# The remainders of the normalised rows: both halves on GpSimd in the closing stages

## The chip, the cores and the metric

The kernel runs on one core of one Trainium2 chip. A core has TensorE (matrix products, transposes), VectorE, ScalarE and GpSimd (elementwise work), and SyncE, whose queue here issues the weight loads. The metric is the device time of one launch in microseconds. Engines run their own instruction streams in order; they meet only at semaphores, on which an instruction waits until a count is reached.

## The reference

One inference step of a backbone with two layers over 640 tokens (128 context tokens, 512 latent tokens, width 1024). Each sub-layer is wrapped in the same chain, and this chain is what the change touches:

```
hp = modulate(rmsnorm(xp, norm_mix_pre[layer]), mod_p[0], mod_p[1])
...                                   # mixer: gMLP + RG-LRU (layer 0), attention (layer 1)
xp = xp + mod_p[2] * rmsnorm(yp, norm_mix_post[layer])
xs = xs + mod_s[2] * rmsnorm(ys, norm_mix_post[layer])
hp = modulate(rmsnorm(xp, norm_ffn_pre[layer]), mod_p[3], mod_p[4])
hs = modulate(rmsnorm(xs, norm_ffn_pre[layer]), mod_s[3], mod_s[4])
xp = xp + mod_p[5] * rmsnorm(sq_relu_mlp(hp, w_ffn_in[layer], w_ffn_out[layer]), norm_ffn_post[layer])
```

All matrix products are of fp32 precision. They are made of three products of a rounded part (type fp32r) and a remainder: high by high, high by low, low by high.

## The kernel before

Tokens are worked on in five tiles of 128 rows (t = 0 to 4). `X` holds the residual stream, `ACC` the sub-layer's sum and later the normalised rows, `HF` the modulated and transposed rows of one token tile in fp32, `HH` its rounded part and `HL` the remainder `HF - HH`, with features on the partitions. `HH` and `HL` are what the next projection multiplies with the weights (`WH`, `WL`, made from `RAW` in a ring of six blocks).

The host code writes one list of steps by hand (`schedule`), and every engine walks through that list and issues its own part of each step, so the list sets the order on every engine. A token tile closes a sub-layer in these steps:

- `post` (ScalarE L859, L860; VectorE L1226, L1228, L1230): mean square of the sub-layer's output, gain, residual add into `X`; signals `x_new`.
- `pre` (ScalarE L869, L870; VectorE L1234, L1235): the norm of `X`, the normalised rows into `ACC`; signals `xn_ready`.
- `T`: TensorE transposes the rows into two PSUM banks (L1602). VectorE evicts the first bank with the modulation into `HF[:, 0:4]` (L1259, four instructions); before that it waits for `h_lo[0]`, the remainder of the first half of the tile before, since there is one `HF`.
- `cut`: ScalarE waits for `h_lo[1]` of the tile before, evicts the second bank into `HF[:, 4:8]` (L890, four instructions), then rounds the halves into `HH` (L895, L897), and signals `h_hi` after each. VectorE forms the remainder of the first half (L1265), GpSimd that of the second (L1058).

`normed(ph, t)` puts these together while the last projection of a sub-layer still runs, two tiles behind: `T` of tile t-2, `post` of t, `cut` of t-2, `pre` of t. Tiles 3 and 4 are left over; `ffn` issues their `T` and `cut` back to back after the first 256 token columns of the first product (`tiles(0, 0)`, which needs the remainders of two tiles), and follows with a modulation product (`mod`, L1544) and the other 384 columns, for which TensorE waits for both halves of all five tiles (`input_ready`, both `h_lo`). There are three closings of this kind: the output projection of layer 0, the last MLP chunk of layer 0, where tiles 3 and 4 are turned between the `qkv` products, and the output projection of layer 1. So each of the three has five cuts, 15 in all.

GpSimd's queue holds, besides the remainders of `HL`, the splits of the weights into `WL` (L1068, two instructions of 128x512 for each block) and, in the attention, the scaling of the weights (L1053), all in the order of the list. ScalarE rounds the weights (L812), and evicts in several stages (L985, L991, L939).

Of the kernel before, what the change touches and what calls it, by code (L numbers as in the profile page):

```python
# [17 lines left out]
P = 128  # L18
# [390 lines left out]
def key_tiles(t):  # L409

    if t == 0:
        return [0]
    return sorted([TT] + list(range(max(1, t - 1), min(LAT, t + 1) + 1)), key=key_slot)
# [17 lines left out]
def hybrid_step(nc, A):  # L431
    f32, f32r, bf16 = mybir.dt.float32, mybir.dt.float32r, mybir.dt.bfloat16
    ALU, ACT, AX = mybir.AluOpType, mybir.ActivationFunctionType, mybir.AxisListType
# [3 lines left out]
    with ctx:  # L437
        def sb(name, shape, dt=f32):
            return ctx.enter_context(nc.sbuf_tensor(name, shape, dt))
# [6 lines left out]
        def sem(name):  # L446
            return ctx.enter_context(nc.semaphore(name))
# [3 lines left out]
        HH = sb("HH", [P, KD, TOK], f32r)  # L451
        HL = sb("HL", [P, KD, TOK], f32r)
# [11 lines left out]
        HF = sb("HF", [P, KD, P])  # L464
# [101 lines left out]
        h_hi = sem("h_hi")  # L566
        h_lo = [sem(f"h_lo{i}") for i in range(2)]
# [65 lines left out]
        def weights_of(i):  # L633

            if i < NKV:
                return GGF[:, 2048 + 512 * i:2560 + 512 * i].rearrange("p (h n) -> p h n", h=4)
            return Z[:, i % 2, :, :]
# [33 lines left out]
        def pt_copies(eng, copy, i, who):  # L671

            for q, (unit, kt, by, _) in enumerate(PT_TILES):
                if unit == i and by == who:
                    upto(eng, pt_mm, q)
                    if i:
                        upto(eng, m_ready, PV_M[i - 1])
                    copy(weights_t(i, kt), PS[:, 4 + q % 2, :]).then_inc(pt_ready[who], 1)  # L678

        def w_view(ld, b):  # L680

            place = raw(ld)
            k = LOADS[ld]["kind"]
            if k == "acols":
                return place.rearrange("p (k n) -> p k n", k=KD)[:, :, P * b:P * b + P]
            return place[:, 1024 * b:1024 * b + 1024]

        def ring_view(buf, ld, j):
            k = LOADS[ld]["kind"]
            if k == "acols":  # L690
                return buf[:, j % RING, :].rearrange("p (k n) -> p k n", k=KD)
            return buf[:, j % RING, :]
# [55 lines left out]
        @block.sync  # L748
        def _(sp):
            for t in range(TT):  # L750
                rows = A["x_prompt"][0] if t == 0 else A["x_sample"][0, (t - 1) * P:t * P, :]
                sp.dma_start(X[:, t, :], rows).then_inc(x_in[t], 16)
            for i, ld in enumerate(LOADS):
                if i in EARLY:
                    sp.dma_start(raw_dst(i, ld), dram_view(ld)).then_inc(early_in[i], 16)
                    continue
                if RAW_NO[i] >= RAWN:

                    old = LOADS[RAW_LD[RAW_NO[i] - RAWN]]
                    if old["kind"] == "mod" and old["vec"] is not None:  # L760
                        sp.wait_ge(vec_read, 4 * old["vec"] + 2 * old["kh"] + 2)
                    elif old["kind"] == "mod" and old["kh"] == 0:
                        sp.wait_ge(mod_read, old["n"] + 1)
                    elif old["kind"] == "mod":
                        upto(sp, m_ready, old["m"])
                    else:
                        sp.wait_ge(w_lo, old["first"] + 2)
                    if i == PT_LOAD + RAWN:
                        upto(sp, m_ready, PV_M[-1])
                sp.dma_start(raw_dst(i, ld), dram_view(ld)).then_inc(raw_in[RAW_NO[i] % RAWN], 16)  # L770

            for t in range(TT):
                sp.wait_ge(x_new, 3 * TT + t + 1)
                dst = A["y_prompt"][0] if t == 0 else A["y_sample"][0, (t - 1) * P:t * P, :]
                sp.dma_start(dst, X[:, t, :]).then_inc(stored, 16)
            sp.wait_ge(stored, 16 * (2 + TT))
            sp.wait_ge(k_out, 16)
# [264 lines left out]
        @block.gpsimd  # L1042
        def _(pool):
            for s in STEPS:
                k = s["kind"]
                if k == "sums":

                    i, z = s["n"], s["n"] % 2
                    nk = P * len(key_tiles(s["t"]))
                    pool.wait_ge(sum_ready, i + 1)  # L1050
                    inv = AST[:, z, 5, :].unsqueeze(2).broadcast_to([P, 4, nk])
                    w = weights_of(i)[:, :, 0:nk]
                    nc.gpsimd.tensor_tensor(w, w, inv, ALU.mult).then_inc(p_ready, 1)  # L1053
                if s["kind"] == "cut":
                    t = s["t"]
                    pool.wait_ge(h_hi, 2 * s["n"] + 2)
                    cols = slice(t * P, t * P + P)
                    nc.gpsimd.tensor_tensor(HL[:, 4:8, cols], HF[:, 4:8, :], HH[:, 4:8, cols].bitcast(f32), ALU.subtract)\  # L1058
                        .then_inc(h_lo[1], 1)
                if k == "B" and s["what"] == "u" and s["t"] == TT - 1:  # L1060
                    pool.wait_ge(h_sum, 3)
                for j, _ in s["split"]:
                    ld, b = BLOCK_LOAD[j]
                    pool.wait_ge(w_hi, j + 1)
                    for piece in (0, 1):
                        cut = (lambda v: v[:, 4 * piece:4 * piece + 4, :]) if LOADS[ld]["kind"] == "acols" else \
                            (lambda v: v[:, 512 * piece:512 * piece + 512])
                        ins = nc.gpsimd.tensor_tensor(cut(ring_view(WL, ld, j)), cut(w_view(ld, b)),  # L1068
                                                      cut(ring_view(WH, ld, j)).bitcast(f32), ALU.subtract)
                    ins.then_inc(w_lo, 1)  # L1070
# [3 lines left out]
        def _(dve):  # L1074
            own = [0]
            V_ = nc.vector
# [70 lines left out]
            for s in STEPS:  # L1147
                k = s["kind"]
# [65 lines left out]
                elif k == "post":  # L1214
                    ph, t = s["ph"], s["t"]
# [15 lines left out]
                elif k == "pre":  # L1231
                    ph, t = s["ph"], s["t"]
# [18 lines left out]
                elif k == "T":  # L1251
                    ph, t, u0 = s["ph"], s["t"], s["m"]
# [6 lines left out]
                        ins = V_.tensor_scalar(HF[:, f, :], m_bank(u0)[:, P * f:P * f + P], MODC[:, layer, off + 1, f, v:v + 1],  # L1259
                                               MODC[:, layer, off, f, v:v + 1], ALU.mult, ALU.add)  # L1260
                    ins.then_inc(m_free[u0 % 2], 1)
                elif k == "cut":
                    cols = slice(s["t"] * P, s["t"] * P + P)
                    dve.wait_ge(h_hi, 2 * s["n"] + 1)
                    V_.tensor_tensor(HL[:, 0:4, cols], HF[:, 0:4, :], HH[:, 0:4, cols].bitcast(f32), ALU.subtract).then_inc(h_lo[0], 1)  # L1265
                elif k == "A":
                    if s["what"] == "xr" and s["fin"] and s["tile"] == 2:
                        conv(dve, V_, link, 0, 0)
# [65 lines left out]
                elif k == "B":  # L1334
                    b, t, nb, what = s["b"], s["t"], s["nb"], s["what"]
# [4 lines left out]
                elif k == "rope":  # L1340

                    t, nb, b = s["t"], s["nb"], s["group"]
                    bank = PS[:, 4 + b % 2, :]
                    heads = 8 if nb < 2 else NKV
                    n = heads * HD
# [35 lines left out]
                elif k == "G2":  # L1381
                    t, c = s["t"], s["c"]
# [55 lines left out]
                elif k == "ya":  # L1438
                    u, t = s["m"], s["t"]
# [4 lines left out]
                elif k == "softmax":  # L1444
                    i, t, z = s["n"], s["t"], s["n"] % 2
# [40 lines left out]
        def _(pe):  # L1486
# [36 lines left out]
            for s in STEPS:  # L1523
# [120 lines left out]
                elif k == "B":  # L1644
                    b, t, nb, what = s["b"], s["t"], s["nb"], s["what"]
                    b_acquire(b)
                    if what == "wout":
                        if s["ph"] == 1 and nb == 0:
                            upto(pe, m_free, YA_M[t])
                        if s["ph"] == 3 and nb == 0:  # L1650
                            upto(pe, m_free, PV_M[NKV * t + 2])
                            upto(pe, m_free, PV_M[NKV * t + 3])
                        if s.get("pt"):
                            before = pv_steps(TT * NKV - 2)
                            for q in (before - 2, before - 1):
                                if q % 2 == b % 2:
                                    _, _, by, count = PT_TILES[q]
                                    pe.wait_ge(pt_ready[by], count)
                    elif what == "qkv":
                        input_ready(pe, TT + (t + 1 if nb == 2 else TT))  # L1660
# [101 lines left out]
                elif k == "PV":  # L1762
# [15 lines left out]
                    def transposed(kt):  # L1778
                        q = base + kt
                        if q >= 2:  # L1780
                            _, _, by, count = PT_TILES[q - 2]
                            pe.wait_ge(pt_ready[by], count)
                        for h in range(4):
                            ins = TR(PS[:, 4 + q % 2, P * h:P * h + P], weights_of(i)[:, h, P * kt:P * kt + P], IDN[:, :])  # L1784
                        ins.then_inc(pt_mm[q % 2], 1)
# [64 lines left out]
```

## Time and profile before

| | |
|---|---|
| median of 3 runs | 1503.34 us (1503.22 to 1504.46) |
| profiled execution | 1500.87 us, span 1499.1 us |
| TensorE busy | 1422.2 us, 95% |
| VectorE, ScalarE, GpSimd busy | 717.2, 545.7, 549.4 us |
| DMA | 153.76 MB, mean 103 GB/s |

The span runs from the first to the last instruction of the profiled execution. Busy is the time in which an engine has an instruction under way; TensorE's instructions overlap each other, so its busy time is not time at its peak.

### The profile page before, as it was taken

Reading aid. Unit: us, or ns where it says so; the run is one execution under the profiler, and the core shown is the slowest. Engines: PE = TensorE matmul, PEld = TensorE weight load, DVE = VectorE, ACT = ScalarE, POOL = GpSimd, SP = SyncE. Lnnn points to the kernel's source line nnn. Section 1 sums busy time; section 2 is a strip of 40 time slices with the busy share of each in tenths; the row PEclk is TensorE's granted clock in tenths of the full one; section 3 lists DMA queues with packets and bytes.
Section 4 is the critical chain, followed back from the end, with each engine's and each line's share of the span. In section 5 each row is a group of like instructions: output and inputs, shape, how many; then the busy total and the mean of one; then the engine's idle time right before and its main releaser. Section 6 shows DMA issues by size and latency. Waiting matters only on the chain.

```text
span 1499.1 us, 19717 instructions
## 1 busy us (share of the span) xinstructions
PE 1422.2 (95%) x7958; PEld 1205.9 (80%) x7958; DVE 717.2 (48%) x1274; ACT 545.7 (36%) x912; POOL 549.4 (37%) x383
## 2 busy tenths in 40 slices
PE   5999999899999999999899889998999999999998
PEld 3876877789889899898667755677989989989986
DVE  5477945532544544545834677617323223222236
ACT  4467706522122122123631466628312212222222
POOL 1431404534244244244334234433624424433430
PEclk8999999999999999999999999999999999999999
DMA  9524253345334234233425000030534213213201
GB/s 353 144 94 143 86 193 104 112 128 112 108 104 141 90 108 141 87 111 119 162 90 170 28 1 1 1 112 29 165 103 127 65 48 113 80 44 103 85 28 71
DMA packets 95026, 153.76 MB, mean 103 GB/s; under 512 B 10764, under 2 KB 49368, under 8 KB 94936
## 3 DMA queue, kind: packets, MB, share of 16 engines
q1 hardware_dynamic: 82432, 145.76, 29.7%
q10 hardware_dynamic: 12504, 6.75, 1.8%
q8 instruction: 63, 1.03, 0.3%
q14 instruction: 27, 0.22, 0.0%
HBM read 149.58 MB, written 2.92 MB: 102 GB/s over the span
## 4 chain that ended last, share of the span: by engine, by line
PE 76%; DVE 8%; ACT 4%; issue 2%; POOL 2%; DMA 2%; DVEq 0%; ACTq 0%
PE PS L1493 23%; PE PS L1495 23%; PE PS L1494 23%; POOL WL L1068 2%; PE PS L1792 1%; PE PS L1784 1%; PE PS L1544 1%; DVE GG L1458 1%; DVE X L1230 1%; PE PS L1642 1%; PE PS L1759 1%; DVE XCB L1226 1%; ACT WH L812 1%; DVE HL L1265 1%; DVE RAW L678 1%
## 5 line engine op out<-in xcount | busy, mean ns | idle before, releaser
L1068 POOL TENSOR_TENSOR WL<-RAW,WH 128x512 fp32r<-128x512 f32 x340 | 468.3, 1413 | 719.3 <-ACT WH L812 701.7
L1493 PE MATMUL PS<-HH,WH 128*128 128x384 f32 (+1 forms) x1152 | 357.9, 311 | 8.4 <-POOL HL L1058 3.6
L1495 PE MATMUL PS<-HH,WL 128*128 128x384 f32 (+1 forms) x1152 | 356.2, 309 | 0.0
L1494 PE MATMUL PS<-HL,WH 128*128 128x384 f32 (+1 forms) x1152 | 356.1, 309 | 0.0
L812 ACT CAST WH<-RAW 128x1024 fp32r<-128x1024 f32 x170 | 169.1, 1047 | 445.3 <-PE PS L1495 331.2
L1493 PE MATMUL PS<-WH,AH 128*128 128x512 f32 x640 | 250.4, 391 | 0.3 <-DVE AL L1282 0.3
L1495 PE MATMUL PS<-WH,AL 128*128 128x512 f32 x640 | 249.5, 390 | 0.0
L1494 PE MATMUL PS<-WL,AH 128*128 128x512 f32 x640 | 249.3, 390 | 0.0
L1493 PEld LDWEIGHTS PS<-HH,WH 128*128 128x128 f32 x1152 | 218.9, 190 | 16.7 <-issue 10.3
L1494 PEld LDWEIGHTS PS<-HL,WH 128*128 128x128 f32 x1152 | 219.1, 190 | 0.6
L1495 PEld LDWEIGHTS PS<-HH,WL 128*128 128x128 f32 x1152 | 218.7, 190 | 0.0
L1301 DVE TENSOR_TENSOR XCB<-XCB 128x640 f32<-128x640 f32 x60 | 70.1, 1168 | 270.7 <-ACT XCB L939 270.4
L1389 DVE TENSOR_TENSOR ACC<-ACC,PS 128x512 f32<-128x512 f32 x140 | 95.8, 686 | 171.8 <-PE PS L1495 171.8
L1493 PEld LDWEIGHTS PS<-WH,AH 128*128 128x128 f32 x640 | 120.2, 188 | 27.4 <-issue 3.3
L1495 PEld LDWEIGHTS PS<-WH,AL 128*128 128x128 f32 x640 | 120.1, 188 | 25.3
L1494 PEld LDWEIGHTS PS<-WL,AH 128*128 128x128 f32 x640 | 120.2, 188 | 24.3
L1493 PE MATMUL PS<-WH,HH 128*128 128x512 f32 x280 | 112.7, 403 | 1.1 <-DVE GG L1353 0.9
L1495 PE MATMUL PS<-WH,HL 128*128 128x512 f32 x280 | 109.9, 393 | 0.0
L1494 PE MATMUL PS<-WL,HH 128*128 128x512 f32 x280 | 109.8, 392 | 0.0
L939 ACT ACTIVATE XCB<-PS 128x640 f32<-128x640 f32 x60 | 42.3, 705 | 163.1 <-PE PS L1495 163.1
L1053 POOL TENSOR_TENSOR GG<-GG,AST 128x1536 f32<-128x1536 f32 (+2 forms) x20 | 55.0, 2748 | 90.3 <-DVE AST L1475 90.3
L1303 DVE TENSOR_TENSOR AL<-XCB,AH 128x640 fp32r<-128x640 f32 x60 | 53.4, 890 | 47.6 <-ACT AH L945 47.6
(210 smaller groups left out, 1624.0 us busy)
## 6 DMA issues: line engine op xcount, KB each, us to landing
RAW<-in_w_mod SPq DMA_DIRECT2D x43, 1024.0 KB, 5.1
RAW<-in_w_ffn_in SPq DMA_DIRECT2D x32, 1024.0 KB, 5.5
RAW<-in_w_ffn_out SPq DMA_DIRECT2D x32, 1024.0 KB, 4.9
RAW<-in_w_in_even SPq DMA_DIRECT2D x7, 1024.0 KB, 5.3
RAW<-in_w_qkv SPq DMA_DIRECT2D x6, 1024.0 KB, 5.2
RAW<-in_w_out_even SPq DMA_DIRECT2D x4, 1024.0 KB, 5.1
GG<-gates ACTq DMA_DIRECT2D x16, 256.0 KB, 3.8
RAW<-in_w_out_odd SPq DMA_DIRECT2D x4, 1024.0 KB, 5.9
```

Of the source, the lines that this page charges most:

```text
L678: copy(weights_t(i, kt), PS[:, 4 + q % 2, :]).then_inc(pt_ready[who], 1)
L812: nc.scalar.copy(ring_view(WH, ld, j), w_view(ld, b)).then_inc(w_hi, 1)
L939: nc.scalar.activation(XC[0], a_bank(a), ACT.Relu).then_inc(a_free[a % 2], 1)
L1053: nc.gpsimd.tensor_tensor(w, w, inv, ALU.mult).then_inc(p_ready, 1)
L1068: ins = nc.gpsimd.tensor_tensor(cut(ring_view(WL, ld, j)), cut(w_view(ld, b)), cut(ring_view(WH, ld, j)).bitcast(f32), ALU.subtract)
L1226: V_.tensor_tensor(YG, ACC[:, t, :], gain, ALU.mult).then_inc(yg_ready, 1)
L1301: V_.tensor_tensor(XC[1], XC[0], XC[0], ALU.mult).then_inc(sq_ready, 1)
L1303: V_.tensor_tensor(AL[:, slot, :], XC[1], AH[:, slot, :].bitcast(f32), ALU.subtract).then_inc(a_lo, 1)
L1389: V_.tensor_tensor(acc, acc, bank, ALU.add).then_inc(b_free[b % 2], 1)
L1493: MM(out, wh, xh, start=first, stop=False)
L1494: MM(out, wh, xl, start=False, stop=False)
L1495: return MM(out, wl, xh, start=False, stop=last)
```

## The change

In every `cut` the remainder of the first half moves from VectorE to GpSimd. GpSimd now waits for the first half's rounding, forms the first remainder, waits for the second rounding and forms the second remainder. VectorE has nothing left in `cut`, neither the wait nor the subtraction. The signals `h_lo[0]` and `h_lo[1]`, and all who wait for them, stay as they are. The steps' order, the number of instructions and the arithmetic are the same.

```diff
@@ gpsimd @@
                 if s["kind"] == "cut":
                     t = s["t"]
+                    cols = slice(t * P, t * P + P)
+                    pool.wait_ge(h_hi, 2 * s["n"] + 1)
+                    nc.gpsimd.tensor_tensor(HL[:, 0:4, cols], HF[:, 0:4, :], HH[:, 0:4, cols].bitcast(f32), ALU.subtract)\
+                        .then_inc(h_lo[0], 1)
                     pool.wait_ge(h_hi, 2 * s["n"] + 2)
-                    cols = slice(t * P, t * P + P)
                     nc.gpsimd.tensor_tensor(HL[:, 4:8, cols], HF[:, 4:8, :], HH[:, 4:8, cols].bitcast(f32), ALU.subtract)\
                         .then_inc(h_lo[1], 1)
@@ vector @@
-                elif k == "cut":
-                    cols = slice(s["t"] * P, s["t"] * P + P)
-                    dve.wait_ge(h_hi, 2 * s["n"] + 1)
-                    V_.tensor_tensor(HL[:, 0:4, cols], HF[:, 0:4, :], HH[:, 0:4, cols].bitcast(f32), ALU.subtract).then_inc(h_lo[0], 1)
```

## Rows read from the trace of the kernel before

**Rows 1.** The page: busy time (share) xinstructions of each engine; the ending chain's shares.
```profile
PE 1422.2 (95%) x7958; PEld 1205.9 (80%) x7958; DVE 717.2 (48%) x1274; ACT 545.7 (36%) x912; POOL 549.4 (37%) x383
...
PE 76%; DVE 8%; ACT 4%; issue 2%; POOL 2%; DMA 2%; DVEq 0%; ACTq 0%
```

**Rows 2.** By source line: the two remainders, min/median/max ns, first and last start.
```profile
L1265 DVE TENSOR_TENSOR HL<-HF,HH x15: 691/1764/1794, 255.4 to 1049.0; 128x512 fp32r<-128x512 f32 x15
...
L1058 POOL TENSOR_TENSOR HL<-HF,HH x15: 1261/1458/1648, 255.2 to 1049.6; 128x512 fp32r<-128x512 f32 x15
```

**Rows 3.** Timeline of VectorE, first closing: start, length, line, [idle before <-releaser].
```profile
257.32 0.76 DVE L1235 TENSOR_SCALAR ACC<-X,STAT 128x1024 f32<-128x1024 f32 x1
...
260.59 1.28 DVE L1230 SCALAR_TENSOR_TENSOR X<-XCB,STAT,X 128x1024 f32<-128x1024 f32 x1
261.79 1.76 DVE L1265 TENSOR_TENSOR HL<-HF,HH 128x512 fp32r<-128x512 f32 x1
263.47 0.15 DVE L1234 RECIPROCAL STAT<-STAT 128x1 f32<-128x1 f32 x1
...
272.74 0.69 DVE L1265 TENSOR_TENSOR HL<-HF,HH 128x512 fp32r<-128x512 f32 x1 [0.69 <-ACT HH L895]
273.47 1.36 DVE L1259 TENSOR_SCALAR HF<-PS,MODC 128x128 f32<-128x128 f32 x4
```

**Rows 4.** Timeline of ScalarE, first closing.
```profile
260.27 0.63 ACT L895 CAST HH<-HF 128x512 fp32r<-128x512 f32 x1
...
261.91 1.06 ACT L869 ACTIVATE GG<-X 128x1024 f32<-128x1024 f32 x1 [0.49 <-DVE X L1230]
...
263.09 0.29 ACT L870 ACTIVATE STAT<-STAT,EPSC 128x1 f32<-128x1 f32 x1
...
274.60 1.51 ACT L890 ACTIVATE HF<-PS,MODC 128x128 f32<-128x128 f32 x4 [1.37 <-POOL HL L1058]
```

**Rows 5.** Timeline of GpSimd, first closing.
```profile
255.20 1.46 POOL L1058 TENSOR_TENSOR HL<-HF,HH 128x512 fp32r<-128x512 f32 x1 [9.87 <-ACT HH L897]
261.50 1.50 POOL L1058 TENSOR_TENSOR HL<-HF,HH 128x512 fp32r<-128x512 f32 x1 [4.84 <-ACT HH L897]
...
273.31 1.26 POOL L1058 TENSOR_TENSOR HL<-HF,HH 128x512 fp32r<-128x512 f32 x1 [3.94 <-ACT HH L897]
277.21 1.26 POOL L1058 TENSOR_TENSOR HL<-HF,HH 128x512 fp32r<-128x512 f32 x1 [2.64 <-ACT HH L897]
```

**Rows 6.** Timeline of TensorE, first closing.
```profile
263.61 0.39 PE L1493 MATMUL PS<-HH,WH 128*128 128x256 f32 x1 [1.66 <-DVE HL L1265]
...
272.20 1.06 PE L1602 MATMUL PS<-IDN,ACC 128*128 128x128 f32 x8 [1.70 <-DVE HF L1259]
274.89 1.92 PE L1544 MATMUL PS<-RAW,CL 128*32 128x512 f32 x16 [1.62 <-DVE HF L1259]
278.62 0.41 PE L1493 MATMUL PS<-HH,WH 128*128 128x384 f32 x1 [1.81 <-POOL HL L1058]
```

**Rows 7.** Timeline of TensorE, third closing.
```profile
1050.97 0.41 PE L1493 MATMUL PS<-HH,WH 128*128 128x384 f32 x1 [1.80 <-POOL HL L1058]
```

**Rows 8.** Timelines of the second closing: VectorE, GpSimd, TensorE.
```profile
749.82 1.59 DVE L1235 TENSOR_SCALAR ACC<-X,STAT 128x1024 f32<-128x1024 f32 x1
...
739.64 12.91 POOL L1068 TENSOR_TENSOR WL<-RAW,WH 128x512 fp32r<-128x512 f32 x8 [2.42 <-ACT WH L812]
...
755.37 0.66 PE L1602 MATMUL PS<-IDN,ACC 128*128 128x128 f32 x4 [1.92 <-ACT HF L890]
756.94 0.50 PE L1493 MATMUL PS<-WH,HH 128*128 128x512 f32 x1 [0.91 <-DVE GG L1353]
```

**Rows 9.** Stretches: busy (x) of PE, PEld, DVE, ACT, POOL; granted clock; DMA.
```profile
280.10:283.50 3.40, 3.40 (x12) 3.40 (x12) 0.00 (x0) 1.01 (x2) 0.00 (x0) 0.50 1.10 365
...
300.00:720.00 420.00, 416.80 (x2367) 372.84 (x2366) 190.70 (x271) 102.71 (x131) 159.87 (x118) 1.00 0.38 118
...
1051.40:1054.80 3.40, 3.40 (x21) 3.40 (x21) 0.00 (x0) 0.88 (x1) 0.00 (x0) 1.00 1.07 360
```

## The prediction

> **What bounds the kernel now.** I read the page first. TensorE is busy 95% of the span and carries 76% of the chain that ended last, VectorE is busy for less than half [rows 1]. So an edit away from TensorE counts only at places where TensorE stands still, and relief of VectorE as such is worth nothing. Next I asked the two remainder lines who waits for them. Both are rare: 15 instructions each in 1499 us [rows 2]. Last I laid the timelines of four engines beside each other in the closings. In the first one TensorE stands four times: 1.66 us for VectorE's remainder of the second tile, then 1.70, 1.62 and 1.81 us round the leftover tiles 3 and 4, the last of them for GpSimd's remainder [rows 6]. The third closing ends in the same stop, 1.80 us [rows 7], the second is built otherwise [rows 8]. In such a stop there is no other work for TensorE, so what happens to the chain of one tile happens to the time.
>
> **Prices.** VectorE's remainder takes 0.69 us when GpSimd is still (the minimum, and the start at 272.74) and up to 1.79 us otherwise [rows 2, 3]. GpSimd's takes 1.26 us when VectorE is still, up to 1.65 us otherwise [rows 2, 5]. The long ones tell how they disturb each other: GpSimd starts at 261.50, inside VectorE's L1230, which ends at 261.87; it ends at 263.00, 1.13 us after that end; VectorE's remainder, issued at 261.79, ends at 263.55, 0.55 us after GpSimd's [rows 3, 5]. They go one after the other. L1235 does the same: 0.76 us alone, 1.59 us while GpSimd splits weights [rows 3, 8]. The evictions L1259, which read PSUM, keep their 1.36 us in both conditions. I take 1.13 to 1.26 us for each GpSimd pass, and let L1226, L1230 and L1235 queue with it.
>
> The Trainium skill ("GPSIMD Engine Reference", section Engine selection) speaks against the change: elementwise work on a tile belongs on VectorE, GpSimd being about twice as slow with two inputs; its measured ratio is 1.96 (section Elementwise). The trace has 1.26 against 0.69 us, 1.83; with the page's ratio a pass would be 1.35 us, and the sum below larger by some 0.1 us for each pass in the chain. It also says ("SBUF — State Buffer", section Who interferes with whom) that the two engines hold their common port for a whole instruction and that the issue order decides who waits; the lengths 0.69 and 1.76 us agree.
>
> **Removed.** VectorE's wait and 15 subtractions. In the running part of a closing the subtraction hides behind ScalarE: after `x_new`, ScalarE makes L869 and L870, which end at 263.38; VectorE's L1265 ends at 263.55 and L1234 follows at 263.47 [rows 3, 4]. Without L1265, L1234 could start at 263.42: 0.05 us a tile gained. I count it as nothing. In cuts 3 and 4 VectorE is idle anyway.
>
> **Added.** GpSimd makes two passes in a row. The first can start as soon as ScalarE's L895 ends, the second follows the first instead of L897. Now in order through the first closing.
>
> Cut 0 (tile 0): the first pass queues behind L1230 of that tile and ends where the only pass ended before, 255.20 + 1.46 = 256.66 [rows 5]. The second takes a further 1.25 us, to 257.9. L1235, ready at 257.24, gets its turn then and ends at 257.9 + 0.55 = 258.46 in place of 257.32 + 0.76 = 258.08 [rows 3]. Everything behind it on VectorE is 0.38 us late.
>
> Cut 1: L895 ends at 260.27 + 0.63 = 260.90 [rows 4], and GpSimd is ready at about 260.98. L1230 would now start at 260.59 + 0.38 = 260.97 [rows 3]. Which comes first is open. Either way two passes and L1230 go in turn: GpSimd first gives 260.98 + 1.26 + 1.08 + 1.16 = 264.5, VectorE first gives 262.26 + 1.16 + 1.25 = 264.7. TensorE needs both halves of tile 1, starts at 264.6 to 264.8 in place of 263.61 [rows 6], 1.0 to 1.2 us late. Besides, the residual rows of tile 3 are ready 0.4 us late (VectorE first) or 1.5 us late (GpSimd first), and ScalarE's L869 with them, which followed them at once [rows 4].
>
> Cut 2: the same turn-taking again. ScalarE's chain puts L895's end at 267.7 to 268.7, and the second pass then ends at 271.3 to 272.0. L1235 of tile 4 gets through after that, at 271.9 to 272.6.
>
> Cut 3: TensorE has turned tile 3 by 271.6 (the stop before 272.20 began at 270.5, one later start of 1.1 us added). L1259 follows L1235 and ends at 273.3 to 273.9; L895 follows that, ends at 273.9 to 274.5, and the two passes at 275.2 to 275.9 and 276.4 to 277.1. Before, the second half was through at 273.31 + 1.26 = 274.57 and released L890 at 274.60 [rows 4, 5].
>
> Cut 4: L890 starts at 276.5 to 277.1, L895 ends 2.0 us later, and two passes of 1.26 us follow: 281.1 to 281.7. TensorE starts 0.15 us later, at 281.3 to 281.9, in place of 278.62 [rows 6]. The `mod` product before it moves from 274.89 to about 277.4 and is done long before. So this closing costs **2.65 to 3.25 us; I take 3.0**. Its parts: about 0.7 us for each of the two leftover cuts, where the second pass now waits for a first of 1.26 us instead of for L897, together 1.5 us; the other 1.5 us come from the turn-taking with L1230 and L1235. The weight loads issued behind `mod` move by 2.5 us, less than TensorE, so they don't bind.
>
> Third closing: the same code, ending in the same stop [rows 7], **3.0 us**.
>
> Second closing: up to cut 7 the turn-taking adds 0.4 and 0.8 us at TensorE, by the rule of cuts 0 and 1 (L1235 behind a second pass). But then TensorE stands 1.92 us for ScalarE's L890 and 0.91 us for VectorE's L1353 [rows 8]. GpSimd is in eight weight splits from 739.64 to 752.55, and both passes of cut 7 now queue behind them: nobody needs them before the third `qkv` tile at 756.94. The second lets L890, and by it the transposes at 755.37, go 0.7 to 1.1 us later. Against that, L1353, which stood behind VectorE's wait for L895 and the subtraction, comes right behind L1259. So 756.94 becomes 756.6 to 757.3: bounds of -0.3 and +0.4 us, I take **+0.1 us**.
>
> **Clock.** After the stops of the first closing TensorE ran a stretch at a granted clock of 0.50 (the 1.2 GHz level): 12 products instead of 21, so 9 x 0.17 = 1.5 us lost; after the same stops in the third it stayed at 1.00 [rows 9]. The new stops are longer (about 2.4 us in place of 1.7). From -1.5 us (the fall comes while TensorE stands) to +4.5 us (one more in each closing); I take half a stretch, **+0.8 us**.
>
> Sum: 3.0 + 3.0 + 0.1 + 0.8 = **+6.9 us**. Against the profiled execution 1500.87 + 6.9 = 1507.8 us (span 1506.0). The median lies 2.47 us above that execution, so I predict 1503.34 + 6.9 = **1510.2 us**. The measurement can tell about 0.2%, 3.0 us, from no change.
>
> **Rivals.**
> - No turn-taking of weight: the passes of GpSimd fit into gaps of VectorE, as the tie in cut 1 leaves open. Then only 0.7 us for each leftover cut stays, 1.5 us a closing, 3.0 us in all, 1506.3 us. For it: L1234 and L1259 aren't disturbed. Against it: L1230 starts within 0.1 us of the first pass.
> - Given back: TensorE is late, but behind the closings it meets waits for ScalarE and weights that don't move and slack eats most; 0 to 2 us stay, 1504.3 us. Against it: between 300 and 720 us TensorE is busy for 416.8 of 420 us [rows 9].
> - The clock falls once more in each closing: 6.1 + 4.5 = 10.6 us, 1513.9 us.
> - Faster: VectorE's queue sets the pace of the closings. Place: between L1230 and L1234 of tiles 2, 3 and 4. Price: the 1.1 us by which the disturbed L1265 exceeds 0.69 us, three tiles, three closings, 9 us, which would give 1494 us. It decides where ScalarE's L870 ends before L1265 does by more than the delay of the second pass. The row has 263.38 against 263.55, so 0.17 us of a price of 1.1; that speaks against it.
>
> **Chances.** Forecast 0.62 (own range 1508 to 1512.5), no turn-taking 0.15, given back 0.10, clock three times 0.07, faster 0.06. The range 1504.8 to 1514.5 leaves out the faster case and half of the given-back one. Slower by over 0.2%: 0.62 + 0.07 + half of 0.15 = 0.77; within 0.2%: 0.17; faster: 0.06.
>
> **What would show it.** On GpSimd 30 passes of `HL`, in cuts 3 and 4 pairs of 1.26 us back to back. TensorE's stop ahead of the 256-column products grows from 1.66 to about 2.7 us, its last stop ends 2.65 to 3.25 us later in relation to the closing's start, and the first and third closings agree. L1230 or L1235 show lengths over 1.5 us in tiles 2 to 4 of the closings. The prediction is wrong if L1230 stays at 1.28 us and L1235 at 0.76 us throughout, or if TensorE's stop at the end of the closing is followed by an earlier end of the next one.

## The result

| | before | after |
|---|---|---|
| median of 4 runs each | 1503.9 us (1503.22 to 1506.61) | 1511.92 us (1511.18 to 1512.64) |
| ratio | | 1.0047, 95% interval 1.0032 to 1.0062 |
| span of the profiled execution | 1499.1 us | 1509.4 us |

The change makes the kernel 8.0 us slower by the medians. The ratio in the table is not the quotient of the medians, which is 1.0053; 1.0047 stands for 7.1 us. In the runs below the two differ by up to 0.0006 as well. The page of after: busy times and the ending chain, the same two lines as [rows 1].

```profile
PE 1426.7 (95%) x7958; PEld 1207.3 (80%) x7958; DVE 697.2 (46%) x1259; ACT 546.9 (36%) x912; POOL 571.4 (38%) x398
...
PE 75%; DVE 8%; ACT 4%; POOL 3%; issue 2%; DMA 2%; DVEq 0%; ACTq 0%
```

VectorE is busy 20 us less, GpSimd 22 us more. That moved work, and TensorE has as many instructions as before (7958); the 8 us are in when things happen. First closing of after, VectorE (the counterpart of [rows 3]; L1238, L1233 and L1262 are the former L1235, L1230 and L1259):

```profile
261.38 1.22 DVE L1238 TENSOR_SCALAR ACC<-X,STAT 128x1024 f32<-128x1024 f32 x1
...
265.12 2.35 DVE L1233 SCALAR_TENSOR_TENSOR X<-XCB,STAT,X 128x1024 f32<-128x1024 f32 x1
...
275.51 1.19 DVE L1238 TENSOR_SCALAR ACC<-X,STAT 128x1024 f32<-128x1024 f32 x1
...
280.01 1.37 DVE L1262 TENSOR_SCALAR HF<-PS,MODC 128x128 f32<-128x128 f32 x4 [2.04 <-POOL HL L1058]
```

GpSimd there (the counterpart of [rows 5]; L1058 is now the first pass, L1061 the second):

```profile
258.82 1.97 POOL L1058 TENSOR_TENSOR HL<-HF,HH 128x512 fp32r<-128x512 f32 x1 [9.36 <-ACT HH L895]
260.76 1.29 POOL L1061 TENSOR_TENSOR HL<-HF,HH 128x512 fp32r<-128x512 f32 x1
265.12 1.27 POOL L1058 TENSOR_TENSOR HL<-HF,HH 128x512 fp32r<-128x512 f32 x1 [3.07 <-ACT HH L895]
266.35 2.25 POOL L1061 TENSOR_TENSOR HL<-HF,HH 128x512 fp32r<-128x512 f32 x1
...
278.71 1.27 POOL L1058 TENSOR_TENSOR HL<-HF,HH 128x512 fp32r<-128x512 f32 x1 [2.56 <-ACT HH L895]
279.94 1.26 POOL L1061 TENSOR_TENSOR HL<-HF,HH 128x512 fp32r<-128x512 f32 x1
```

The taking of turns is plain to see. At 265.12 GpSimd's first pass and VectorE's L1233 start in the same hundredth; the pass takes its undisturbed 1.27 us, L1233 takes 2.35 in place of 1.28 us, and then the second pass takes 2.25 us behind it. ScalarE and TensorE (the counterpart of [rows 4, 6]; TensorE's first line is tile 2's transposes, from which closings are measured below):

```profile
267.50 1.06 ACT L869 ACTIVATE GG<-X 128x1024 f32<-128x1024 f32 x1 [1.94 <-DVE X L1233]
...
281.23 1.51 ACT L890 ACTIVATE HF<-PS,MODC 128x128 f32<-128x128 f32 x4 [2.08 <-POOL HL L1061]
...
289.49 2.01 ACT L812 CAST WH<-RAW 128x1024 fp32r<-128x1024 f32 x2 [5.73 <-DMA RAW<-in_w_ffn_in]
293.93 1.99 ACT L812 CAST WH<-RAW 128x1024 fp32r<-128x1024 f32 x2 [2.42 <-DMA RAW<-in_w_ffn_in]
```

```profile
265.03 1.03 PE L1601 MATMUL PS<-IDN,ACC 128*128 128x128 f32 x8
...
268.69 0.36 PE L1492 MATMUL PS<-HH,WH 128*128 128x256 f32 x1 [2.63 <-issue]
...
278.12 1.94 PE L1601 MATMUL PS<-IDN,ACC 128*128 128x128 f32 x8 [2.56 <-DVE HF L1262]
281.44 3.54 PE L1543 MATMUL PS<-RAW,CL 128*32 128x512 f32 x16 [1.37 <-DVE HF L1262]
285.97 0.41 PE L1492 MATMUL PS<-HH,WH 128*128 128x384 f32 x1 [0.99 <-POOL HL L1061]
...
296.78 0.35 PE L1492 MATMUL PS<-HH,WH 128*128 128x256 f32 x1 [2.25 <-ACT XCB L939]
```

The same starts in before, first and last landmark of [rows 6] extended:

```profile
260.91 1.03 PE L1602 MATMUL PS<-IDN,ACC 128*128 128x128 f32 x8
...
288.95 0.36 PE L1493 MATMUL PS<-HH,WH 128*128 128x256 f32 x1 [0.18 <-issue]
```

Three things stand here. The closing takes 285.97 - 265.03 = 20.94 us against 278.62 - 260.91 = 17.71, 3.23 more, and the third closing repeats it (20.95 against 17.71). The `mod` products take 3.54 us against 1.92: they run at the low clock. And TensorE now stops for 2.25 us at the next pair of tiles (296.78), for ScalarE's L939, which stood behind the rounding of weights that had come late. That stop isn't in before (0.18 and 0.49 us there, first and third closing). In the third closing of after it is short, and for another engine, GpSimd's split of the weights:

```profile
1070.39 0.35 PE L1492 MATMUL PS<-HH,WH 128*128 128x256 f32 x1 [0.70 <-POOL WL L1071]
```

The 10.3 us between the two spans aren't all of the change. At 265.03 the profiled execution of after is already 4.1 us late, and no `cut` comes before 258 us. Two stretches of low clock lie earlier; before has none there:

```profile
76.60:79.90 3.30, 3.30 (x7) 2.15 (x7) 3.09 (x7) 1.07 (x1) 0.00 (x0) 0.50 0.00 0
117.60:120.90 3.30, 3.30 (x8) 2.07 (x7) 0.83 (x1) 3.25 (x4) 0.00 (x0) 0.50 0.00 0
```

So below a closing is compared with a closing, within one execution, and the whole by medians and ratios.

### The profile page after: what moved, and what is told of

It reads as the page before. It is cut to its first block, busy times and chain, and to the rows that moved or that the text cites. A ratio compares the mean times of both kernels' runs of the same rounds, so it can differ in the third digit from the quotient of the medians.

```text
span 1509.4 us, 19717 instructions
## 1 busy us (share of the span) xinstructions
PE 1426.7 (95%) x7958; PEld 1207.3 (80%) x7958; DVE 697.2 (46%) x1259; ACT 546.9 (36%) x912; POOL 571.4 (38%) x398
## 4 chain that ended last, share of the span: by engine, by line
PE 75%; DVE 8%; ACT 4%; POOL 3%; issue 2%; DMA 2%; DVEq 0%; ACTq 0%
PE PS L1492 22%; PE PS L1494 22%; PE PS L1493 22%; POOL WL L1071 2%; PE PS L1543 1%; PE PS L1791 1%; PE PS L1783 1%; DVE X L1233 1%; DVE GG L1457 1%; DMA RAW<-in_w_ffn_in 1%; DVE HF L1262 1%; ACT GG L869 1%; PE PS L1641 1%; DVE XCB L1229 1%; PE PS L1758 1%
## 5 line engine op out<-in xcount | busy, mean ns | idle before, releaser
L939 ACT ACTIVATE XCB<-PS 128x640 f32<-128x640 f32 x60 | 42.3, 705 | 165.7 <-PE PS L1494 165.7
```

Source lines behind the costliest of these rows:

```text
L939: nc.scalar.activation(XC[0], a_bank(a), ACT.Relu).then_inc(a_free[a % 2], 1)
```

## The experiments

For each profiled execution the table gives starts on TensorE's timeline, counted from the first of tile 2's transposes: `mod`, the 384-column products ("end") and the 256-column products of the next pair of tiles ("next"); first / third closing, us.

| kernel | mod | end | next | ratio to before (95%) |
|---|---|---|---|---|
| before | 13.98 / 13.99 | 17.71 / 17.71 | 28.04 / 26.79 | |
| after | 16.40 / 16.42 | 20.94 / 20.95 | 31.75 / 30.22 | 1.0047 (1.0032 to 1.0062) |
| leftover | 14.61 / 14.60 | 19.13 / 19.12 | 30.13 / 28.87 | 1.0021 (1.0009 to 1.0033) |
| running | 15.77 / 16.30 | 19.50 / 20.02 | 30.93 / 29.08 | 1.0022 (1.0013 to 1.0032) |
| second | 14.00 / 13.99 | 17.73 / 17.71 | 29.20 / 28.67 | 1.0000 (0.9986 to 1.0013) |
| order | 18.67 / 17.50 | 23.19 / 22.02 | 33.92 / 32.33 | 1.0050 (1.0038 to 1.0063) |
| vector_both | 14.29 / 14.29 | 17.86 / 17.83 | 29.51 / 28.90 | 1.0004 (0.9987 to 1.0020) |
| vector_leftover | 14.48 / 14.48 | 18.05 / 17.36 | 30.62 / 28.25 | 1.0014 (1.0002 to 1.0027) |
| before_warm | 15.17 / 15.17 | 19.72 / 19.72 | 28.13 / 28.13 | 0.9985 (0.9974 to 0.9996) |
| both_warm | 15.61 / 15.61 | 18.38 / 18.38 | 28.31 / 28.37 | 0.9987 (0.9975 to 0.9998) |
| before_warm2 | 14.00 / 14.00 | 17.73 / 17.74 | 26.72 / 28.12 | 0.9985 (0.9973 to 0.9998) |
| after_warm | 16.39 / 16.40 | 20.92 / 20.93 | 29.32 / 29.33 | 1.0011 (1.0000 to 1.0022) |
| both_warm2 | 14.29 / 14.28 | 16.48 / 16.47 | 27.00 / 27.00 | 0.9984 (0.9974 to 0.9994) |

My theory: a pass of GpSimd lies in the chain of each leftover cut, and in the running cuts its passes take turns with VectorE's L1230 and L1235. Rivals: one of the two alone; a first pass behind the weight splits; the clock.

### The change in parts: leftover, running, second

The first pass on GpSimd only for some cuts `s["n"]`, on VectorE as before for the others.

```diff
# leftover: (3, 4, 13, 14); running: (0, 1, 2, 10, 11, 12); second: 5 to 9
+                    if s["n"] in (3, 4, 13, 14):
+                        pool.wait_ge(h_hi, 2 * s["n"] + 1)
+                        nc.gpsimd.tensor_tensor(HL[:, 0:4, cols], ...).then_inc(h_lo[0], 1)
...
+                    if not (s["n"] in (3, 4, 13, 14)):
+                        dve.wait_ge(h_hi, 2 * s["n"] + 1)
+                        V_.tensor_tensor(HL[:, 0:4, cols], ...).then_inc(h_lo[0], 1)
```

> The change in four cuts only, those of tiles 3 and 4 in the first and the third closing; the other eleven keep VectorE's remainder. Measure of a closing: from the start of tile 2's transposes to the start of the 384-column products, 17.71 us before and 20.94 us with the whole change. My theory (two passes in a row cost 0.7 us in each leftover cut, queueing with L1230 and L1235 the rest): 19.15 us a closing, +1.45, so +2.9 us in all, ratio 1.0019. Rival (the two passes in a row carry the whole price): 20.9 us, ratio near 1.005. Rival (clock falls and other executions' scatter make the difference): no relation, ratio 1.000 with a closing of 17.7.

> The complement within the first and the third closing: the change in the six cuts of tiles 0 to 2 only. My theory (GpSimd's two passes and VectorE's L1230 and L1235 take turns, and the residual rows of tiles 3 and 4 come late): the stop ahead of the 256-column products grows from 1.66 to 2.6 us, the closing is 19.5 us, +1.8, in all +3.6 us, ratio 1.0024. Rival (no turn-taking of weight, running cuts are hidden): closing 17.7 to 17.9 us, ratio 1.000.

> The change in the five cuts of the second closing only (last MLP chunk of layer 0 and the qkv products behind it). My theory: the passes queue behind eight weight splits, but TensorE's third qkv tile waits for VectorE's L1353, which now comes earlier, so from the last transposes of tile 2 to the third qkv tile it takes 16.2 to 17.3 us against 16.95 before: ratio 0.9998 to 1.0003. Rival (a first pass behind eight splits is what TensorE ends up waiting for): 2 to 3 us more, ratio 1.0015 to 1.002.

Measured: leftover 19.13 us where 19.15 was expected, running 19.50 in the first closing where 19.5 was expected. In the third closing running took 20.02, with a low clock from 1042 us on. 1.42 + 1.79 = 3.21 us, the whole change has 3.23: the two halves add up and neither carries the closing's price alone. The ratios fit, 1.0021 x 1.0022 x 1.0000 = 1.0043 against 1.0047, but each of them is uncertain by about 0.001 and holds the clock's part as well. The halves are not equal everywhere: the start of `mod`, which turns out to matter below, moves by 0.63 us in leftover and by 1.79 in the first closing of running, together 2.42 as in after. The stop ahead of the 256 columns is 1.67 us in leftover and 2.61 us in running.

In the second closing nothing is to be measured, as expected (ratio 1.0000). The timelines of after show why (VectorE, GpSimd; the counterpart of [rows 8]):

```profile
761.38 1.36 DVE L1262 TENSOR_SCALAR HF<-PS,MODC 128x128 f32<-128x128 f32 x4 [2.42 <-POOL HL L1058]
762.66 0.42 DVE L1352 COPY GG<-PS 128x256 f32<-128x256 f32 x1
...
747.63 12.48 POOL L1071 TENSOR_TENSOR WL<-RAW,WH 128x512 fp32r<-128x512 f32 x8 [1.19 <-ACT WH L812]
760.06 1.28 POOL L1058 TENSOR_TENSOR HL<-HF,HH 128x512 fp32r<-128x512 f32 x1
761.30 1.26 POOL L1061 TENSOR_TENSOR HL<-HF,HH 128x512 fp32r<-128x512 f32 x1
```

Both passes wait behind eight splits and VectorE stands 2.42 us for the first, but the eviction that frees the bank for the third `qkv` tile (L1352) follows L1262 at once instead of standing behind a wait for ScalarE.

### Who goes first: order

```diff
+                    if t < 3 and s["ph"] != 2:
+                        pool.wait_ge(x_new, (s["ph"] - 1) * TT + t + 3)
                     pool.wait_ge(h_hi, 2 * s["n"] + 1)
```

> The changed kernel, but in the six cuts of tiles 0 to 2 of the first and the third closing GpSimd also waits for VectorE's residual rows of tile t+2 (x_new) before its first pass, so L1230 goes first. My theory (the passes take turns with L1230, and whose turn is first sets how late the next tile's residual rows are): L1230 is 1.28 us everywhere in place of 2.35 us, the stop ahead of the 256-column products stays at 2.6 to 2.8 us, and the closing takes 20.3 to 20.4 us in place of 20.94, ratio 1.0039 where the change had 1.0047. Rival (only the lengths of the two passes count): 20.9 us or more, since the first pass now starts later.

A miss; the rival's condition came true. VectorE's and TensorE's timelines of the run (L1235 is the former L1230, L1264 the former L1259):

```profile
261.58 1.28 DVE L1235 SCALAR_TENSOR_TENSOR X<-XCB,STAT,X 128x1024 f32<-128x1024 f32 x1
...
274.69 1.37 DVE L1264 TENSOR_SCALAR HF<-PS,MODC 128x128 f32<-128x128 f32 x4 [1.75 <-PE PS L1603]
...
265.53 0.55 PE L1494 MATMUL PS<-HH,WH 128*128 128x256 f32 x1 [3.22 <-issue]
...
273.98 1.04 PE L1603 MATMUL PS<-IDN,ACC 128*128 128x128 f32 x8
```

The residual add does keep its 1.28 us. But TensorE's stop grew to 3.22 us, not 2.6 to 2.8: the pass that used to be queued now starts after a signal. And the 256-column products that follow take 273.98 - 265.53 = 8.45 us against 5.85 in before, at the low clock. The first pass comes later than in after (4.25 against 3.66 us from tile 2's transposes to the 256 columns), and the low clock delays tile 3's transposes, for which VectorE's L1264 waits 1.75 us, 0.58 in the third closing. My estimate without these waits is 23.19 - 1.75 and 22.02 - 0.58, 21.44 us for both closings, 0.5 us over after. So letting L1230 go first gains nothing here: what it wins on VectorE is lost again by the later first pass.

### The mirror: vector_both, vector_leftover

VectorE forms both remainders, everywhere or in the four leftover cuts; GpSimd's part goes.

```diff
                     V_.tensor_tensor(HL[:, 0:4, cols], HF[:, 0:4, :], HH[:, 0:4, cols].bitcast(f32), ALU.subtract).then_inc(h_lo[0], 1)
+                    dve.wait_ge(h_hi, 2 * s["n"] + 2)
+                    V_.tensor_tensor(HL[:, 4:8, cols], HF[:, 4:8, :], HH[:, 4:8, cols].bitcast(f32), ALU.subtract).then_inc(h_lo[1], 1)
```

> The mirror of the change: VectorE forms both remainders in all 15 cuts, GpSimd none. My theory (the pass's length on its engine is in the chain of a closing, and VectorE's passes of 0.69 us undisturbed are the shorter ones): first and third closing 16.5 us, 1.2 less than before, and in the second closing ScalarE's L890 is no longer behind eight weight splits on GpSimd, 1 to 1.4 us less; in all -3.4 to -3.8 us, ratio 0.9976. Rival (VectorE is what closings wait for, relief of it is right and only GpSimd's slowness spoils the change): the running cuts get longer, closing 17.7 to 19 us, ratio 1.000 to 1.002.

> Before, but VectorE forms both remainders in the four leftover cuts of the first and the third closing. The chain of semaphores gives 0.58 us less for each leftover cut, 16.5 us a closing instead of 17.71. Theory after the run with both on VectorE everywhere: the products of mod (L1543 there) run at the low clock, 3.6 us instead of 1.9, and end after the remainders, so the closing ends at 17.3 to 17.9 us and the gain is lost; ratio 0.999 to 1.0005. Rival (what was lost there came from the running cuts): 16.5 us, ratio 0.9984.

Both gained nothing. vector_both has 1.0004 where 0.9976 was expected, vector_leftover with 1.0014 is beyond the expected 1.0005 and slower than before: in it `mod` starts 0.5 us later, since VectorE's second pass now stands ahead of tile 4's eviction (L1259 of before), on which `mod` waits. VectorE and TensorE in the first closing of vector_both:

```profile
279.17 0.68 DVE L1264 TENSOR_TENSOR HL<-HF,HH 128x512 fp32r<-128x512 f32 x1
...
277.81 3.64 PE L1543 MATMUL PS<-RAW,CL 128*32 128x512 f32 x16 [2.10 <-DVE HF L1256]
293.04 0.36 PE L1492 MATMUL PS<-HH,WH 128*128 128x256 f32 x1 [2.20 <-ACT XCB L939]
```

The remainders are complete at 279.85, 16.3 us after the transposes: the chain is as short as I had worked out. But TensorE is in `mod` at the low clock until 281.4, and then again stops 2.2 us for L939. That raised two questions, what the clock takes and what the next pair of tiles hangs on.

### TensorE kept busy: before_warm, both_warm

In the first and the third closing TensorE gets products of the identity for its four stops: 10, 10, 10 and 12 in before_warm, 8, 12, 12 and 4 in both_warm, which is vector_both otherwise. They write a PSUM bank that is free at that time, and nobody reads them.

```diff
+            def busy(b, n):
+                upto(pe, b_free, b)
+                for _ in range(n):
+                    MM(PS[:, 4 + b % 2, 0:P], IDN[:, :], IDN[:, :], start=True, stop=True)
...
+                    if prev["kind"] == "cut" and prev["ph"] != 2:      # after mod
+                        busy(s["b"] - 2, 12)
...
+                    if s["ph"] != 2 and t > 1:                         # after T of tiles 2, 3, 4
+                        busy(s["b"] - 2, {2: 10, 3: 10, 4: 10}[t])
```

> Before, with 42 additional products of the identity (128 columns, into a PSUM bank that is free) for TensorE's four stops in the first and in the third closing; their results are not used. If the low clock in and behind the closings comes from TensorE's standing, there is none there: the 384-column products at 278.62 run at the full clock. The closing's length stays 17.71 us (its chain isn't TensorE's). Gain at most 1.5 us in the first closing, and less where the weight loads behind mod come next: ratio 0.999 to 1.000. Rival (the low clock has nothing to do with the stops): low stretches as before, ratio 1.000; the products delay the transposes: ratio 1.001.

> Both remainders on VectorE in all cuts, with 36 additional products of the identity in each of the first and the third closing, as in the run before_warm. Theory (the low clock in mod took the gain away): mod takes 1.9 to 2.0 us, the closing 16.4 to 16.6 us. But mod starts no earlier than before (0.3 us later in the run without the products), so the weight loads behind it come no earlier and TensorE waits for ScalarE's L939 behind them by what it won; in all 0 to -2 us from these closings and up to -1.4 us from the second: ratio 0.9980 to 1.000. Rival (VectorE's two passes cost as much as they give): closing 17.7 us also at the full clock, ratio 1.000 to 1.001.

The products took 0.24 us each, too long for their number: they delayed the transposes, and the closing of before_warm ends at 19.72 us, 2.0 later than in before; that of both_warm takes 18.38 where 16.4 to 16.6 was expected. Yet both kernels are faster than before (0.9985, 0.9987). So a later end of the closing can go with a faster kernel. There was no stretch of low clock in the two closings of either run, and `mod` took 1.92 us; second and vector_leftover, whose stops aren't filled, have low clock in both closings on the same chip.

The next pair shows two ways. In before_warm it starts at 28.13 us without a stop, 8.41 us after the closing's end: TensorE goes from the 384-column products straight into it. In both_warm it starts at 28.31 us after a stop of 1.36 us for L939, 12.70 us after `mod`'s start.

### The three designs at full clock: before_warm2, after_warm, both_warm2

The same with counts that fit the stops: 6, 6, 6, 7 for before; 10, 10, 9, 9 for the changed kernel; 3, 8, 8, 0 for both remainders on VectorE.

> Before, with fewer additional products than in before_warm (6, 6, 6 and 7 in the four stops of each of the two closings, 0.24 us each by that run), so that they fit into the stops of 1.66, 1.70, 1.62 and 1.81 us and don't delay the transposes. Theory: the closing is 17.7 us, no low clock in it, mod starts 14.0 us after tile 2's transposes and the next pair of tiles 26.8 us after them (28.1 us in before_warm, where mod started at 15.2): the way from mod over the weight loads to ScalarE's L939 binds, 12.8 us. Ratio 0.9975 to 0.9985. Rival (the gain of before_warm came from anything else): the next pair stays at 28 us, ratio 0.9985.

> The changed kernel with such products in the same two closings (10, 10, 9 and 9 in the stops). Theory: the change's price in the chain doesn't need the low clock. Closing 20.9 to 21.0 us, mod at 16.4 us after tile 2's transposes, the next pair of tiles at 29.2 us, that is 2.4 us more per closing than before_warm2, 4.8 us in all: ratio to before 1.0010 to 1.0018, to before_warm2 1.003. Rival (most of the price is the low clock that longer stops bring): no difference from before_warm2, ratio 0.998.

> Both remainders on VectorE in all 15 cuts, with 3, 8 and 8 additional products in the first three stops of the two closings. Theory: closing 16.3 to 16.5 us, mod at 14.3 us, mod takes 1.92 us, and the next pair of tiles at 27.1 us, since it hangs on mod's start and not on the closing's end; ratio 0.9975 to 0.9990, the same as before_warm2 within its interval. Rival (the closing's end binds): the next pair 1.2 us earlier than in before_warm2, ratio 0.9965 to 0.9975.

TensorE and ScalarE in before_warm2, first closing, then the third:

```profile
276.93 1.92 PE L1552 MATMUL PS<-RAW,CL 128*32 128x512 f32 x16 [0.29 <-DVE HF L1259]
...
289.65 0.35 PE L1493 MATMUL PS<-HH,WH 128*128 128x256 f32 x1 [0.42 <-ACT XCB L939]
...
283.91 2.00 ACT L812 CAST WH<-RAW 128x1024 fp32r<-128x1024 f32 x2 [4.74 <-DMA RAW<-in_w_ffn_in]
286.79 2.00 ACT L812 CAST WH<-RAW 128x1024 fp32r<-128x1024 f32 x2 [0.88 <-DMA RAW<-in_w_ffn_in]
288.70 0.70 ACT L939 ACTIVATE XCB<-PS 128x640 f32<-128x640 f32 x1
...
1055.41 2.00 ACT L812 CAST WH<-RAW 128x1024 fp32r<-128x1024 f32 x2 [4.79 <-DMA RAW<-in_w_ffn_in]
1059.65 1.99 ACT L812 CAST WH<-RAW 128x1024 fp32r<-128x1024 f32 x2 [2.24 <-DMA RAW<-in_w_ffn_in]
```

`mod` reads the last of `RAW`, the load of the next weights follows, ScalarE rounds them, and only then comes to L939, which frees TensorE's bank. From `mod`'s start to the next pair it is 12.72 us, and 14.12 in the third closing, where the second load came 1.4 us later behind the first (why is open). That third closing is as the rival had it (the next pair at 28 us), and so is the ratio, 0.9985; this run alone doesn't part theory and rival. TensorE, after_warm and then both_warm2:

```profile
279.92 1.92 PE L1551 MATMUL PS<-RAW,CL 128*32 128x512 f32 x16 [0.24 <-DVE HF L1262]
281.77 2.27 PE L1525 MATMUL PS<-IDN 128*128 128x128 f32 x18
284.45 0.41 PE L1492 MATMUL PS<-HH,WH 128*128 128x384 f32 x1 [0.40 <-POOL HL L1061]
...
292.85 0.28 PE L1492 MATMUL PS<-HH,WH 128*128 128x256 f32 x1
```

```profile
277.39 1.92 PE L1549 MATMUL PS<-RAW,CL 128*32 128x512 f32 x16 [0.32 <-DVE HF L1256]
279.58 0.41 PE L1492 MATMUL PS<-HH,WH 128*128 128x384 f32 x1 [0.27 <-DVE HL L1264]
290.10 0.36 PE L1492 MATMUL PS<-HH,WH 128*128 128x256 f32 x1 [1.94 <-ACT XCB L939]
```

after_warm: the closing takes 20.92 us without any low clock in it, so the 3.2 us are the chain's alone. The next pair is at 29.3 us, without a stop, 8.40 us after the closing's end. It is 2.6 and 1.2 us later than in before_warm2, 3.8 in all; the medians of the same chip are 1507.14 and 1503.99 us, 3.15 apart (1.0021; 4.8 us or 1.003 was expected). both_warm2: the closing ends at 16.48, 1.25 us earlier than in before_warm2, and TensorE hands all of it back in a stop of 1.94 us for L939; the next pair at 27.0, ratio 0.9984 against 0.9985. The rival, that the closing's end binds in before_warm2, falls.

With the stops filled, the next pair starts at the later of two times: 8.4 us after the closing's end, or about 12.7 us after `mod`'s start. The first binds in before_warm and after_warm, the second in before_warm2, both_warm and both_warm2; nine of the ten closings fit within 0.1 us, the tenth is the third of before_warm2. In before_warm2's first closing the closing's end alone would have given 17.74 + 8.4 = 26.1 us, so 0.6 us of a closing can be hidden there.

before_warm, both_warm, before_warm2 and both_warm2 are 0.13 to 0.16% under before by the ratios, 1.4 to 2.0 us by the medians. Nothing here says that VectorE's second remainder adds to it.

## Why the prediction was right

1510.2 us was predicted (+6.9), 1511.92 measured (+8.0 by the medians, +7.1 by the ratio), inside the range. The mechanism, a longer chain in two closings, is shown. The total is in part luck, as two terms were wrong in opposite directions.

- **Prices.** Passes of 1.26 to 1.29 us undisturbed, 1.97 to 2.25 us in turn; L1230 2.35 us, L1235 1.19 and 1.22 us; L1259 stays at 1.35 to 1.37. As said, for the reason given.
- **Cut 0 and cut 1.** L1235 of tile 2 ends 0.40 us later, counted from tile 2's transposes (0.38 predicted). The tie in cut 1 fell to GpSimd, and TensorE's stop grew by 0.97 us (1.0 to 1.2 predicted).
- **The closing.** 3.23 and 3.24 us (2.65 to 3.25 predicted, 3.0 taken). The two parts of the sum, 1.5 us from the leftover cuts and 1.5 from the turn-taking, were measured apart at 1.42 and 1.79. The first rival, no turn-taking of weight, is out.
- **Second closing.** +0.1 was taken. From tile 2's transposes (746.24, 754.33 in after) to the third `qkv` tile (756.94, 764.57) it went from 10.70 to 10.24 us, just beyond the bound of -0.3, and 0.44 us were lost ahead of it: from the `mod` products at 729.55 and 737.20 to the third `qkv` tile it is 27.39 us in before, 27.37 in after and 27.37 in second, whose ratio is 1.0000.
- **Weight loads.** Here a step failed: "The weight loads issued behind `mod` move by 2.5 us, less than TensorE, so they don't bind." They do move by 2.4 us, less than TensorE, and in after_warm they don't bind. But they bind already in the kernel without the change: before_warm2's next pair stands for L939, and so the first 0.6 us by which the closing gets longer cost nothing there. The profile of before hid it: in the first closing the low clock behind the stop held TensorE back until the weights were there [rows 9], and in the third the stop for L939 was 0.49 us. With the second load late in one of the two closings of before_warm2, 3.15 us (medians) to 3.8 us (timelines) are left at full clock in place of 6.1.
- **Clock.** +0.8 us was taken, on the picture that a low stretch comes behind the stops. In after it came inside the closing, in both:

```profile
277.95:284.70 6.75, 5.21 (x24) 2.17 (x24) 1.39 (x5) 3.68 (x8) 3.86 (x4) 0.50 0.02 5
1052.80:1059.50 6.70, 4.86 (x24) 2.16 (x24) 1.69 (x6) 3.72 (x9) 3.51 (x3) 0.50 0.01 2
```

It didn't lengthen the closing. It took its price by `mod`'s 3.54 us, from which the weights are late: SyncE's two issues of these loads take 1.98 us in the first closing of after, 1.23 in after_warm, and ScalarE's second rounding follows the first after 4.44 us, 2.87 in after_warm. The next pair is 2.4 us (first closing) and 0.9 us (third) later than in after_warm, 3.3 in all, where before against before_warm2 has 1.3 and -1.3. The term was too small. By the medians +8.0 against 3.15 us leaves 4.9 us to the clock, by the ratios +7.1 against 3.9 us leaves 3.2 us, each uncertain by more than 3 us from the intervals. How much of this is the change's is not settled, since kernels whose closings are those of before fall too. Nor does the clock of the whole span tell: it has a mean of 0.985 in the four executions of after, and of 0.986 to 0.987 in the 27 to 35 of before that the later runs were compared with, but 0.990 in the profiled one, which was a favourable execution. In the run second, whose first closing is unchanged, `mod` took 3.64 us, and TensorE stopped for L939 (its `mod`, its next pair, its clock from 276.1 on):

```profile
277.13 3.64 PE L1549 MATMUL PS<-RAW,CL 128*32 128x512 f32 x16 [1.62 <-DVE HF L1263]
292.33 0.36 PE L1498 MATMUL PS<-HH,WH 128*128 128x256 f32 x1 [2.02 <-ACT XCB L939]
...
276.10:282.80 6.70, 5.58 (x22) 2.57 (x23) 2.36 (x6) 2.53 (x6) 1.97 (x2) 0.50 0.34 89
```

Taking the sum against one profiled execution made the closings of before look faster than they mostly are: 28.04 and 26.79 us to the next pair there, 29.20 and 28.67 in second. It also left out the low stretch behind the second closing of before (granted clock 0.50 from 758.0 to 761.4 us), which after doesn't have. The total came out near the truth because two errors had opposite signs, a chain counted at 6.1 us that is worth 3 to 4, and a clock counted at 0.8 us that is worth more.

- **The faster rival** (VectorE sets the pace) is out: relieved of 20 us it gained nothing, and L1234 still starts on ScalarE's signal, 1.55 us after VectorE falls idle. Its price was added up wrongly, too: 1.1 us x 9 is 9.9 us, not 9.

## What to carry to other kernels

When an engine in a chain gets a second pass, count what its passes do to the other engine's neighbours as well: 1.79 of the closing's 3.2 us came from the cuts in which VectorE's own instructions had to take turns with GpSimd. After costing a closing by its end, follow the transfers that were issued inside it. Here the next work hung on the later of the closing's end and the start of a small product that freed a buffer, and a closing shorter by 1.25 us gave nothing. And compare local lengths within an execution; two executions differed by 4 us before the first changed instruction.

## What was not expected of the hardware

- TensorE's granted clock fell to 0.50 (the 1.2 GHz level) after a row of stops of 1.6 to 2.6 us with short work between them, in or right behind 15 of the 16 first and third closings of the eight kernels with unfilled stops (not in the third of before); where it fell on `mod`, that took 2.95 to 3.64 us instead of 1.92. With the stops filled by products nobody reads, it fell in neither closing of before_warm, both_warm, before_warm2 and after_warm; in both_warm2 it fell only behind the stops of 1.94 us for L939, while in both_warm it didn't after such stops of 1.36 and 1.42 us.
- GpSimd's and VectorE's instructions with the same start (265.12) didn't share: one took 1.27 us, the other 2.35 in place of 1.28. The Trainium skill ("SBUF — State Buffer", section Who interferes with whom) has an exclusive hold for the whole instruction; the trace agrees, and puts GpSimd first in this tie.
- The products of the identity took 0.24 us each for 128 columns, as two records each in the trace.
